# Index scores of a streaming encoder step: units of up to 1024 keys, prompt tiles first, sample units spread among them

## The reference, cut to what matters

```python
def dsa_attend(q, qi, wi, qpos, k_all, v_all, ki_all, k_sel):
    ...
    s = jnp.einsum('bqhd,bld->bqhl', qi.astype(F32), ki_all.astype(F32)) * IDX_DIM ** -0.5
    score = jnp.einsum('bqh,bqhl->bql', wi.astype(F32) * IDX_HEADS ** -0.5, jax.nn.relu(s))
    chunk_end = (qpos // CHUNK + 1) * CHUNK - 1
    admissible = kpos[None, :] <= chunk_end[:, None]
    score = jnp.where(admissible[None], score, -jnp.inf)
    top_val, top_idx = lax.top_k(score, k_sel)
    ...
```

## Time and profile before

| what | us |
|---|---|
| median of 3 runs | 3117.33 (3112.48 to 3118.05) |
| span of the profiled execution | 3115.3 |
| TensorE busy | 2719.6 (87%) |
| VectorE busy | 2179.2 (70%) |
| ScalarE busy | 1100.6 (35%) |
| GpSimd busy | 634.8 (20%) |

### The profile page before, as it was taken

How to read it: one execution, slowest core, us unless ns; L and a number is a source line. 1 busy time by engine, 2 the same in 40 slices (tenths; PEclk the granted TensorE clock), 3 DMA queues, 4 the chain that set the end, 5 groups by cost and what they waited for, 6 DMA issues and landing times. The chain is left out here.

```text
span 3115.3 us, 40926 instructions
## 1 busy us (share of the span) xinstructions
PE 2719.6 (87%) x15348; PEld 2279.6 (73%) x15398; DVE 2179.2 (70%) x3768; ACT 1100.6 (35%) x1970; POOL 634.8 (20%) x694
## 2 busy tenths in 40 slices
PE   6879969999998999996577775899999986599998
PEld 4667539999998888996465653667777765488886
DVE  2326999999999999997688855666666655344333
ACT  2215971112221212212544442555554443232222
POOL 0002002333333333433044532211111000000000
PEclk8869989999999999998699987999999998799999
DMA  5320015222225233346412415211110005522221
GB/s 183 134 83 1 1 58 170 87 89 88 87 87 189 88 102 95 97 142 218 177 41 68 122 45 169 72 41 41 31 31 28 21 20 167 186 93 98 92 81 48
DMA packets 177409, 286.03 MB, mean 92 GB/s; under 512 B 27834, under 2 KB 125890, under 8 KB 173382
## 3 DMA queue, kind: packets, MB, share of 16 engines
q1 hardware_dynamic: 157401, 220.56, 22.4%
q0 software_dynamic: 19824, 62.97, 5.4%
HBM read 177.77 MB, written 105.71 MB: 91 GB/s over the span
## 5 line engine op out<-in xcount | busy, mean ns | idle before, releaser
L705 DVE TENSOR_SCALAR_CACHE_REDUCE project_junk<-all_S,project_cand 128x528 bf16<-128x528 f32 (+7 forms) x256 | 370.0, 1445 | 4.8 <-DVE project_cand L730 4.7
L629 PE MATMUL PS<-project_wh,project_xh 128*128 128x256 f32 x1224 | 348.0, 284 | 8.6 <-POOL project_wl L675 5.7
L629 PE MATMUL PS<-project_xh,project_wh 128*128 128x384 f32 (+1 forms) x880 | 317.0, 360 | 37.9 <-DMA project_xl<-x_parts 37.9
L629 PE MATMUL PS<-project_wl,project_xh 128*128 128x256 f32 x1224 | 347.6, 284 | 0.0
L629 PE MATMUL PS<-project_wh,project_xl 128*128 128x256 f32 x1224 | 347.4, 284 | 0.0
L1601 DVE TENSOR_TENSOR attend_ptl<-PS,attend_pth 128x512 fp32r<-128x512 f32 x272 | 186.3, 690 | 186.9 <-ACT attend_pth L1539 186.0
L629 PE MATMUL PS<-project_xh,project_wl 128*128 128x384 f32 (+1 forms) x880 | 316.3, 359 | 0.0
L629 PE MATMUL PS<-project_xl,project_wh 128*128 128x384 f32 (+1 forms) x880 | 316.0, 359 | 0.0
L705 DVE TENSOR_SCALAR_CACHE_REDUCE project_tie<-all_S,project_cand 128x384 bf16<-128x384 f32 (+6 forms) x224 | 315.7, 1409 | 0.0
L675 POOL TENSOR_TENSOR project_wl<-project_raw,project_wh 128x1024 fp32r<-128x1024 f32 x80 | 201.6, 2541 | 240.4 <-ACT project_wh L642 240.4
L1539 ACT CAST attend_pth<-PS 128x512 fp32r<-128x512 f32 x272 | 157.8, 585 | 242.2 <-PE PS L1486 241.2
(11 more groups left out here) (309 smaller groups left out, 6026.8 us busy)
## 6 DMA issues: line engine op xcount, KB each, us to landing
project_raw<-in_w_in SPq DMA_DIRECT2D x80, 512.0 KB, 4.4
featT<-project_st POOLq DMA_DIRECT2D x66, 192.0 KB, 2.2
featT<-project_st POOLq DMA_DIRECT2D x44, 256.0 KB, 2.3
gate_s<-project_st POOLq DMA_DIRECT2D x68, 128.0 KB, 2.1
gate_a<-project_st POOLq DMA_DIRECT2D x68, 128.0 KB, 2.2
x_conv<-all_S SPq DMA_DIRECT2D x8, 1088.0 KB, 5.3
conv_x<-x_conv SPq DMA_DIRECT2D x8, 1088.0 KB, 6.6
ssd_zs<-gate_s SPq DMA_DIRECT2D x17, 512.0 KB, 4.4
```

What stands on the lines that cost most here:

```text
L629: last = nc.tensor.matmul(PS[:, r % 8, 0:w], lhsT, rhs, start=(k == 0 and j == 0), stop=(k == KT - 1 and j == 2))
L705: v.tensor_scalar((junk, tie)[j % 2][:, 0:L], tile_scores(j), th, None, op, ALU.add, accum_out=into[:, j:j + 1]).then_inc(counted, 1)
```

## The change: what it does

- An item may have up to 1024 columns. Tiles 2 to 7 are one item each, in pairs; tiles 8 to 15 are cut in two halves. 22 prompt items, 176 prompt units. A unit of over 512 columns is written as two halves into two neighbouring PSUM banks (4 matmuls), read by one relu instruction and accumulated by one VectorE instruction.
- PSUM is used as three slots of two banks (`NSLOT = 3`), banks 0 to 5; banks 6 and 7 are for transposes. TensorE may be three units ahead of ScalarE. There are still 4 relu buffers, of 1024 columns now.
- Prompt units come first. The sample tile is one item of 528 columns, 8 units of 32 matmuls; one of them is put in the middle of each of the third to the tenth group of 16 prompt units (from tiles 6 and 7 to tile 14).
- The cached keys are loaded twice, beside each other, so that one transpose gives the keys on both halves of the partitions; the high copy and the subtraction are one instruction of 128 rows each. Sequence s is transposed behind unit 10 + 2s, the parameters behind unit 26.
- The cached keys, the parameter rows and `qpad` lie in the end of `S`, which the last prompt tiles overwrite later.

```diff
-        relu = m("relu", [P, 4, 512])
         kiS = m("kiS", [P, 2, NB, LS], F32R)
-        qpad = m("qpad", [P, 2, NB, P], F32R)
-        kc = S[:, SALL - 2048:SALL].rearrange("p (n c) -> p n c", c=ID)
+        relu = m("relu", [P, 4, 1024])
+        qpad = b.map("scores_pad", b.s_end - 4 * 2 * NB * P)("qpad", [P, 2, NB, P], F32R)
+        kc_at = SALL - 2 * NB * P - 2 * 2048
+        kc = S[:, kc_at:kc_at + 2 * 2048].rearrange("p (n r d) -> p n r d", r=2, d=ID)
+        rows = S[0:CONV_ROWS, kc_at - CONVC:kc_at]
...
-        items = [(t, c, w) for t in SEL for c, w in even_pieces(keys_of(t))]
-        units = [(item, h, len(items[i:i + 2])) for i in range(0, len(items), 2)
-                 for h in range(IH) for item in items[i:i + 2]]
+        def halves(t):
+            n = t + 1
+            if n <= 1024 // P:
+                return [(t, 0, n * P)]
+            return [(t, 0, n // 2 * P), (t, n // 2 * P, (n - n // 2) * P)]
+        groups = [[(t, 0, keys_of(t)) for t in (t0, t0 + 1)] for t0 in range(SEL0, 8, 2)]
+        groups += [halves(t) for t in range(8, TILES)]
+        for j, items in enumerate(groups):
+            started.append(len(units))
+            block_ = [(item, h) for h in range(IH) for item in items]
+            if 2 <= j < 2 + IH:
+                block_.insert(len(block_) // 2, ((ST, 0, LS), j - 2))
+            units += block_
+        turn_at = {10 + 2 * s: s for s in range(NB)}
+        PAR_AT = 10 + 2 * NB
+        NSLOT = 3
+        def cut(w):
+            return (1, w) if w <= 512 else (2, w // 2)
...
             @block.sync
-                sp.dma_start(kc, b.cache_kidx.rearrange("b (k p) d -> p (b k) d", p=P)).then_inc(kc_in, 16)
+                for r in range(2):
+                    sp.dma_start(kc[:, :, r, :], b.cache_kidx.rearrange("b (k p) d -> p (b k) d", p=P)
+                                 ).then_inc(kc_in, 16)
...
             @block.tensor
+                def turn_keys(s):
+                    pe.wait_ge(kc_in, 32)
+                    wait(pe, kc_lo, s - 1)
+                    for i in range(4):
+                        last = nc.tensor.transpose(PS[:, 6 + s % 2, i * P:(i + 1) * P],
+                                                   kc[:, 4 * s + i].rearrange("p r d -> p (r d)"), b.ident[:, :])
+                    last.then_inc(kc_turned, 1)
+                def turn_rows():
+                    pe.wait_ge(rows_in, 48)
+                    pe.wait_ge(kc_lo, NB - 1)
...
+                for n, ((t, c0, w), h) in enumerate(units):
+                    wait(pe, relu_done, n - NSLOT + 1)
...
+                        for i in range(e):
                             for part in range(2):
+                                last = nc.tensor.matmul(out(n, w)[:, i, :], b.qs[:, h, t * P:(t + 1) * P],
+                                                        b.ks[:, part, c0 + i * hw:c0 + (i + 1) * hw],
+                                                        start=(part == 0), stop=(part == 1))
                     last.then_inc(sim_ready, 1)
+                    if n in turn_at:
+                        turn_keys(turn_at[n])
+                    if n == PAR_AT:
+                        turn_rows()
...
             @block.scalar
+                    if n in turn_at:
+                        s = turn_at[n]
+                        act.wait_ge(kc_turned, s + 1)
+                        nc.scalar.copy(kiS[:, 0, s, 0:PAST], PS[:, 6 + s % 2, :]).then_inc(kc_hi, 1)
...
             @block.vector
+                    if n in turn_at:
+                        s = turn_at[n]
+                        dve.wait_ge(kc_hi, s + 1)
+                        v.tensor_tensor(kiS[:, 1, s, 0:PAST], PS[:, 6 + s % 2, :], kiS[:, 0, s, 0:PAST], ALU.subtract
+                                        ).then_inc(kc_lo, 1)
```

More of the change, by code:

```diff
@@ new lines, in stage_scores @@
+        groups += [halves(t) for t in range(8, TILES)]
+        units = []
+        started = []
+        for j, items in enumerate(groups):
[4 more added lines that the diff above has]
+            units += block_
+        TAIL = next(j for j, items in enumerate(groups) if 4 * (SOFF[items[-1][0]] + keys_of(items[-1][0])) >
+                    4 * (kc_at - CONVC))
@@ new lines, in stage_scores, with out @@
+        sample = [n for n, ((t, _, _), _) in enumerate(units) if t == ST]
+        turn_at = {10 + 2 * s: s for s in range(NB)}
+        PAR_AT = 10 + 2 * NB
+        assert PAR_AT < sample[0] and sample[-1] < started[-1]
+        before = {}
+        for n, (item, h) in enumerate(units):
+            before[n] = max([i for i in range(n) if units[i][0] == item], default=-1)
+        NSLOT = 3
+        def cut(w):
+            return (1, w) if w <= 512 else (2, w // 2)
+        def out(n, w):
+            e, hw = cut(w)
+            s = 2 * (n % NSLOT)
+            return PS[:, s:s + e, 0:hw]
@@ L405, in _ @@
                     last.then_inc(kc_turned, 1)
[L406 to L413, removed]
@@ L414, in _ @@
-                for n, ((t, c0, w), h, _) in enumerate(units):
-                    wait(pe, relu_done, n - 7)
-                    out = PS[:, n % 8, 0:w]
-                    if t == ST:
-                        pe.wait_ge(pad_done, n + 1)
-                        for s in range(NB):
-                            for part in range(2):
[L421 to L427, removed]
+                def turn_rows():
+                    pe.wait_ge(rows_in, 48)
+                    pe.wait_ge(kc_lo, NB - 1)
+                    for f in range(CONVC // P):
+                        last = nc.tensor.transpose(PS[:, 6, f * CONV_ROWS:(f + 1) * CONV_ROWS],
+                                                   rows[:, f * P:(f + 1) * P], b.ident[0:CONV_ROWS, 0:CONV_ROWS])
+                    last.then_inc(par_turned, 1)
@@ L451, in _ @@
                                   ).then_inc(new_done, 1)
[L452 to L458, removed]
+                for n, ((t, c0, w), h) in enumerate(units):
+                    if n == started[TAIL]:
+                        dve.wait_ge(par_turned, 1)
                     acc = S[:, SOFF[t] + c0:SOFF[t] + c0 + w]
@@ L477, in _ @@
                 pool.wait_ge(pad_zero, 1)
[L478 to L480 removed]
+                for h in range(IH):
+                    if h >= 2:
+                        pool.wait_ge(sim_ready, sample[h - 2] + 1)
                     for s in range(NB):
[L482 to L483 removed]
+                        last = nc.gpsimd.tensor_copy(qpad[:, h % 2, s, s * NT:(s + 1) * NT],
+                                                     b.qs[:, h, SEQ + s * NT:SEQ + (s + 1) * NT])
                     last.then_inc(pad_done, 1)
```

47 lines of the change are left out of this document (27 added, 20 removed).

## The result

The changed kernel takes 3066.23 us (median of 4 runs, 3060.58 to 3071.07) against 3116.29 us before (4 runs, 3112.48 to 3118.05; three of them stand in the table of before). The ratio is 0.9845, 95% interval 0.983 to 0.9859: 50 us, 1.5%, faster. Forecast were 3065.8 us.

What follows compares the result with a forecast made beforehand. VectorE's accumulations bound the prompt part, the key transfer and TensorE's sample units earlier parts. 1.4 + 156.9 + 5.2 + 4.0 + 5.6 + 7.5 = 180.6 us of stage, 51.5 less: time 3065.8 us, range 3060 to 3073.

Steps and rivals of the forecast that it cites:

- the start: Start of the scores stage: TensorE begins at 219.1 without waiting for loads, VectorE at about 220.4, 1.4 us in.
- VectorE's work: Scores stage: 156.9 us for prompt units after 16.2 saved, 5.2 for sample units, 5.6 for eight cached-key subtractions.
- waits around the sample units: Tiles 8 to 14: TensorE's group sums exceed VectorE's by 2.8 us; with sample units not quite absorbed, 4 us.
- waits in the stretch of the keys: First transposes, behind unit 10: second key copy lands at about 231; 5.2 us waiting plus clock losses, together 7.5 us.
- The bound of each part: Scores stage before: part one the cached keys' transfer, part three TensorE (sample units), part four VectorE's accumulations (prompt units).
- rival C: Prompt units: wide accumulations cost by the 2048-column row, 12 us more, time 3078; chance 0.05.
- rival E: Prompt units: accumulation's fixed part is smaller, 112 fewer instructions save 8.3 us, not 14.4, time 3072; chance 0.03.
- The clock's two parts: Around the wait for the keys: TensorE at half clock costs 1.1 us before the wait and 1.2 after it.
- TensorE busy without a wait in tiles 8 to 14: Groups with sample units in tiles 8 to 14: sign that TensorE becomes the bound, by 2.8 us in sum.
- Rival B: Tiles 8 to 14: TensorE bounds in earnest, each matmul 15% dearer, 16 us more, time 3082; chance 0.10.
- Rival A: Scores stage: second key copy lands in time, sample matmuls hide wholly; gain 62 us, time 3056; chance 0.14.
- Rival D: Scores stage: TensorE falls to half clock and stays there; stage ends at about 500, time 3166; chance 0.02.

Runs made afterwards that it cites:

- e3_narrow: The changed kernel with items of at most 512 columns, 38 prompt items in pairs, sample units in eight of 19 groups; stage 212.7 us, time 3094.42 us.
- e1_late_turns: The changed kernel with the cached keys' transposes behind units 20 to 34 instead of 10 to 24, parameters behind unit 36; stage 178.2 us, time 3055.32 us.
- e2_late_pool: As e1_late_turns, with GpSimd's zeroing of the padded queries waiting until 8 units are out of TensorE; stage 178.4 us, time 3058.42 us.
- e4_block: The changed kernel with the 8 sample units in one block ahead of tile 15 instead of spread over eight groups; stage 200.7 us, time 3077.65 us.
- e5_high_only: The changed kernel without the sample units' matmuls against the low part of the keys, 16 a unit instead of 32; stage 189.3 us, time 3071.41 us.
- e7_halves: The changed kernel with each sample unit cut in two of 264 columns, at one and three quarters of the group; stage 187.3 us, time 3066.97 us.
- e9_narrow_six: e3_narrow with six slots of one bank instead of three of two, and sample units cut in two of 264 columns; stage 197.5 us, time 3078.66 us.

## Why the prediction was right, point by point

The time came within 0.5 us, the stage within 2.2: VectorE ended 182.8 us into it, not 180.6. The nearness of the time is partly luck, since runs of one kernel differ by 10 us. So is that of the sum, in which errors of up to 1.6 us have both signs. Against the forecast: the start 1.5 us (1.4); VectorE's work 168.7 (156.9 + 5.2 + 5.6 = 167.7), of which 1.4 is the multiplication beside the memset that no term had; waits around the sample units 5.6 (4.0); waits in the stretch of the keys 6.6 (7.5 with the clock); 0.4 in small gaps.

- The bound of each part, read from the waits, held: the two stretches that waited for the keys and for TensorE's sample units went, and the prompt part lost its fixed costs. Width measured alone gives 16.8 us of VectorE's busy time (e3_narrow) for the forecast 16.2. (One price in it was misread: the two rows of the first head's multiplication, 0.39 and 0.315 us, give 0.09 fixed and 0.59 ns a column, not 0.112 and 0.543; on 16 items that is 0.35 us.) The step of 1024 columns is 1.196 us as worked out, so rival C (wide accumulations dearer) and rival E (a smaller fixed part) fall, and with E the Trainium skill's 58 cycles, 60 ns (VectorE: DVE Perf Modes, the section on the TRN2 errata): 129 ns an instruction was the right figure here.
- The start: VectorE began 1.54 us into the stage (1.4 forecast). The second copy was there 13.3 us after the issue, not 12; VectorE waited 6.1 us for it, not 5.2. e1_late_turns took out 5.9 us, so of the 7.5 forecast for this term the wait is nearly all that moving the transposes gives back. The clock's two parts: before the wait the forecast 1.1 us is what e2_late_pool shows (0.54 + 0.34 + 0.21), but in the changed kernel the long multiplication covers it. After the wait, where the clock was 0.50 until 234, I had 1.2 us; the small waits there are 0.55 us in all (0.18, 0.20 and 0.17).
- The sample units: 4.6 us at seven accumulations, and with those at the prompt units beside them 5.6, against 4. The sign "TensorE busy without a wait in tiles 8 to 14" did not come: its weight loads waited 4.2 us there for ScalarE to free banks. With three slots TensorE could not use its whole time. That fits what the 4 us were short of, though no run isolates it: sample accumulations are 13.6 us apart from tile 8 to tile 9 and 14.9 from tile 10 to tile 11, where my sums for TensorE give 12.9 and 14.7. Rival B (15% more for each matmul, 15 us or more of waits) falls with the 5.6 us, and e4_block shows the same 3.9 us a sample unit. Rival A fell with the first wait.
- Rival D: the granted clock was 1.0 from 236 us on, at a higher TensorE load than before.
- GpSimd's part was wrong in kind. I wrote that it has a whole group's time for the next pads; e5_high_only shows that it may get no turn in a whole group. In the changed kernel its copies were harmless, 1.7 to 5.2 us for eight. They begin when TensorE ends a sample unit, and there VectorE mostly had a pause, since TensorE's time for the unit wasn't covered: the copies at 277.76 begin inside the pause before 278.38, and the first one at 260.73 ends 0.06 us into the pause at 261.99. That the pause is what saved them is read from these times and from e5_high_only, where it was missing; no run tests it alone. If it is so, the sum came out right only since that pause was in it.

## What to carry to other kernels

Where one engine is the bound of one part and another of the next, lay the parts side by side: spreading the sample units was worth 16.5 us here, as much as the fixed costs saved by width. Put the foreign unit where its length is covered by stored work, and count stored work in microseconds, not in buffers. A wait that stands in an engine's order holds everything behind it, so put work on a late transfer as far back as its consumer allows. When a pause of VectorE is removed, ask who lived on it: small GpSimd copies beside a full VectorE should go to ScalarE or be done ahead.

## What the runs showed of the hardware

- A GpSimd copy of 128x16, 0.19 us by itself, lasted up to 31.1 us while VectorE issued its instructions without a pause, most of them accumulations with two operands in SBUF, and ended when VectorE paused. The Trainium skill (SBUF — State Buffer, the section on who interferes with whom) has such a VectorE instruction contend with a GpSimd instruction that reads SBUF. The trace agrees, and goes further: 36 VectorE instructions began within the copy of 29.8 us and 35 within that of 31.1, and GpSimd got no turn between them. Line of e5_high_only's copies, shortest, median and longest in ns:

```profile
L528 POOL CAST scores_pad_qpad<-index_qs x64: 192/194/31107, 220.3 to 344.1; 128x16 fp32r<-128x16 f32 x64
```

- Not every copy fares so. Two lines of the kernel after, near the start of the stage:

```profile
219.83 6.58 POOL L530 CAST scores_pad_qpad<-index_qs 128x16 fp32r<-128x16 f32 x16
220.29 5.37 DVE L507 SCALAR_TENSOR_TENSOR all_S<-scores_relu,all_wi,all_S 128x384 f32<-128x384 f32 x9
```

  VectorE has no pause from 220.29 to 225.66 either, and yet GpSimd gets one copy done for each accumulation; it lasts 0.58 us beside one of 384 columns and 0.72 beside one of 512. The five copies of 9.2 to 31.1 us (two in e5_high_only, two in e7_halves, one in e9_narrow_six) were each the first after GpSimd had been idle; a copy right behind another was never held for more than one VectorE instruction. But other first copies got their turn at once (0.30 us at 312.05 in e7_halves), so what decides is open.
- VectorE's one-operand multiplication of 384 columns took 1.79 us beside GpSimd's memset of 1.80 us and 0.42 without it, the other way round: here GpSimd was first. Beside two-operand accumulations the memset held nobody up: 1.81 us at 226.06 in e2_late_pool, with accumulations of 0.61 and 0.75 us.
- A PSUM read across two banks by one ScalarE instruction costs no more than its columns: 1.029 us for 1024, where the fit to one bank (0.84 ns a column) had given 1.03.
